# The division in the memory softmax of a two-layer decoder, moved from VectorE to ScalarE

## The reference

```python
def memory_branch(q_mem, mem, norm_mem, w_mem_kv):
    k_m, v_m = jnp.split(rmsnorm(mem, norm_mem) @ w_mem_kv, 2, axis=-1)
    q, k, v = _heads(q_mem, N_MEM_HEADS), _heads(k_m, N_MEM_HEADS), _heads(v_m, N_MEM_HEADS)
    sc = jnp.einsum('bqhd,bkhd->bhqk', q, k).astype(jnp.float32) * HEAD_DIM ** -0.5
    p = jax.nn.softmax(sc, axis=-1)
    o = jnp.einsum('bhqk,bkhd->bqhd', p.astype(v.dtype), v)
    return o.reshape(q_mem.shape)
```

## Time and profile before

| | |
|---|---|
| median of three runs | 1313.81 us (1313.54 to 1314.25) |
| profiled execution | 1317.49 us |
| its span, first to last instruction | 1315.7 us |
| TensorE busy | 1236.4 us, 94% |
| VectorE busy | 794.0 us, 60% |
| ScalarE busy | 555.4 us, 42% |
| GpSimd busy | 105.6 us, 8% |
| mean granted clock of TensorE | 0.976 |

### The profile page before, as it was taken

The page is one execution under the profiler, slowest core; times in us unless marked ns, Lnnn a source line. Parts: engine busy times, 40 slices in busy tenths (PEclk is TensorE's granted clock), DMA queues, the critical chain, the costliest instruction groups (busy, mean ns, idle before and its releaser), DMA issues.

```text
span 1315.7 us, 16934 instructions
## 1 busy us (share of the span) xinstructions
PE 1236.4 (94%) x5975; PEld 1014.6 (77%) x5975; DVE 794.0 (60%) x1235; ACT 555.4 (42%) x918; POOL 105.6 (8%) x133
## 2 busy tenths in 40 slices
PE   5889999989999999999999897777999999999998
PEld 4767888768788888878887676666878888887886
DVE  4866666654777777732267566554477777775225
ACT  5536656644444444421254442423344444442223
POOL 0201333332000000000020000000300000000000
PEclk9989999999999999999999897898999999999999
DMA  7412121113333333323321221111333333332642
GB/s 227 129 32 64 50 65 49 49 41 89 97 96 96 96 96 96 97 95 97 127 64 52 61 67 47 49 49 33 97 88 100 98 97 96 96 96 82 161 123 83
DMA packets 183893, 112.50 MB, mean 86 GB/s; under 512 B 20063, under 2 KB 176031, under 8 KB 183839
## 3 DMA queue, kind: packets, MB, share of 16 engines
q1 hardware_dynamic: 183838, 111.79, 28.9%
HBM read 107.58 MB, written 2.10 MB: 83 GB/s over the span
## 4 chain that ended last, share of the span: by engine, by line
PE 83%; DVE 11%; ACT 3%; issue 2%; DMA 1%; POOL 0%; SPq 0%; DVEq 0%; ACTq 0%; POOLq 0%
PE bank L1281 17%; PE bank L1283 17%; PE bank L1282 17%; PE bank L1569 7%; PE bank L1542 7%; PE bank L1433 2%; PE bank L1434 2%; PE bank L1435 2%; DVE w_lo L848 2%; PE bank L1555 2%; PE bank L1491 2%; PE bank L1582 1%; PE bank L1691 1%; PE bank L1469 1%; PE bank L1509 1%
## 5 line engine op out<-in xcount | busy, mean ns | idle before, releaser
L1281 PE MATMUL bank<-y_hi,w_hi 128*128 128x512 f32 x928 | 367.6, 396 | 2.8 <-DVE w_lo L848 2.5
L1282 PE MATMUL bank<-y_lo,w_hi 128*128 128x512 f32 x928 | 363.2, 391 | 0.0
L1283 PE MATMUL bank<-y_hi,w_lo 128*128 128x512 f32 x928 | 363.1, 391 | 0.0
L556 ACT ACTIVATE w_hi<-raw 128x1024 fp32r<-128x1024 f32 x186 | 196.5, 1056 | 355.5 <-PE bank L1283 180.1
L848 DVE TENSOR_TENSOR w_lo<-raw,w_hi 128x1024 fp32r<-128x1024 f32 x188 | 229.9, 1223 | 160.3 <-ACT w_hi L556 157.7
L1281 PEld LDWEIGHTS bank<-y_hi,w_hi 128*128 128x128 f32 x928 | 175.5, 189 | 41.8 <-issue 4.7
L1282 PEld LDWEIGHTS bank<-y_lo,w_hi 128*128 128x128 f32 x928 | 175.5, 189 | 37.0 <-issue 1.2
L1283 PEld LDWEIGHTS bank<-y_hi,w_lo 128*128 128x128 f32 x928 | 175.3, 189 | 36.9
L1542 PE MATMUL bank<-ar,w_hi 128*128 (+1 forms) x288 | 88.8, 389 | 0.8 <-DVE af L1066 0.8
L715 ACT ACTIVATE af<-af,conv 128x512 f32<-128x512 f32 x88 | 63.0, 716 | 36.0 <-DVE af L1066 36.0
L1569 PE MATMUL bank<-w_hi,ar 128*128 128x512 f32 x288 | 77.1, 390 | 0.8 <-DVE af L1066 0.8
(11 more groups left out here) (189 smaller groups left out, 1638.1 us busy)
## 6 DMA issues: line engine op xcount, KB each, us to landing
raw<-in_a_ffn_up SPq DMA_DIRECT2D x44, 512.0 KB, 3.8
raw<-in_b_ffn_up SPq DMA_DIRECT2D x44, 512.0 KB, 3.8
raw<-in_a_ffn_down SPq DMA_DIRECT2D x22, 512.0 KB, 3.3
raw<-in_b_ffn_down SPq DMA_DIRECT2D x22, 512.0 KB, 3.7
raw<-in_a_w_in SPq DMA_DIRECT2D x20, 512.0 KB, 3.8
raw<-in_w_kv_shared SPq DMA_DIRECT2D x12, 512.0 KB, 3.9
raw<-in_a_w_out SPq DMA_DIRECT2D x8, 512.0 KB, 3.8
raw<-in_b_w_in SPq DMA_DIRECT2D x8, 512.0 KB, 3.9
```

The costliest lines, as they stand in the source:

```text
L556: nc.scalar.activation(w_hi[:, m % SPLIT, :], raw[:, m % RAW, :], ACT.Copy).then_inc(hi_done, 1)
L1281: mm(bank, w[0], y[0][:, k, :], start=(k == 0), stop=False)
L1282: mm(bank, w[0], y[1][:, k, :], start=False, stop=False)
L1283: last = mm(bank, w[1], y[0][:, k, :], start=False, stop=(k == KT - 1))
```

## The change

The four multiplications leave VectorE. VectorE takes the reciprocals and signals them by a new semaphore `mrcp`; ScalarE waits for it directly behind its four exponentials, and then does four copies of 128 x 256 in place, with the reciprocal as scale. The last copy raises `mpn`. Before the reciprocals of a later head VectorE waits for the copies of the head before. The place in the program of everything else stays.

```diff
+        mrcp = sem("mrcp")
...
                     nc.scalar.activation(pm[:, M * qt:M * (qt + 1)], banks[2 + qt // 2][:, M * (qt % 2):M * (qt % 2) + M],
                                          ACT.Exp, bias=st[:, 8 + qt:9 + qt],
                                          accum_out=st[:, 12 + qt:13 + qt]).then_inc(mexp, 1)
+                act.wait_ge(mrcp, i + 1)
+                for qt in range(TT):
+                    ins = nc.scalar.activation(pm[:, M * qt:M * (qt + 1)], pm[:, M * qt:M * (qt + 1)], ACT.Copy,
+                                               scale=st[:, 16 + qt:17 + qt])
+                ins.then_inc(mpn, 1)
...
                     dve.wait_ge(mexp, 4 * (i + 1))
-                    link(nc.vector.reciprocal(st[:, 16:20], st[:, 12:16]))
-                    for qt in range(TT):
-                        ins = nc.vector.tensor_scalar(pm[:, M * qt:M * (qt + 1)], pm[:, M * qt:M * (qt + 1)],
-                                                      st[:, 16 + qt:17 + qt], None, ALU.mult)
-                    ins.then_inc(mpn, 1)
+                    if i:
+                        dve.wait_ge(mpn, i)
+                    nc.vector.reciprocal(st[:, 16:20], st[:, 12:16]).then_inc(mrcp, 1)
```

## The result

The changed kernel takes 1319.70 us (median, 1319.15 to 1320.30), the kernel before 1313.81 in the same comparison: ratio 1.0039, 95% interval 1.0026 to 1.0051, so 3.4 to 6.7 us slower (the two medians alone differ by 5.9 us, or 1.0045). Two later comparisons gave 1.0070 (1.0055 to 1.0085) and 1.0049 (1.0036 to 1.0063). The sign and the size of some 6 us hold in all three; the first two intervals don't overlap, and why is a part of what follows.

A forecast was written before the change was run, and what follows sets the result against it. The chain of waits, mostly on VectorE and ScalarE, was taken to bound the memory stretches, TensorE what follows. Layer B's 3.3 plus layer A's 2.5 gave 5.8 us, added to the median 1313.8: 1319.6 us; range 1316.0 to 1323.5.

The forecast's parts named there:

- layer A's term: Layer A's four slots: delays of 0.25, 0.91, 0.51 and 0.90 us, 2.5 us at the last head's values.
- The price of a copy: ScalarE's scaled 128 x 256 copies: 0.40 us from start to start, 0.50 for one; four have landed after 1.70.
- The slots with a tile: Where a filling tile ends, `w_lo` waits for ScalarE's delayed copy to `w_hi`: t + 2.90, some 0.90 to 1.03 us later.
- The slots without: Where no tile ends, TensorE's transposes wait for the probabilities: t + 1.92 instead of t + 1.41, 0.51 us later.
- Layer B: Layer B's four slots: delays of 0.90, 0.51, 0.90 and 1.03 us, together 3.3 us.
- rival 1: Longer pause before layer A's slot 3 transposes lowers TensorE's clock: 2 us more or somewhat over, 1321.5 to 1323; chance 0.18.
- The clock in layer B: Layer B's low-clock stretch may cover less of the work behind the pauses: up to 2 us back, 1317.6; chance 0.12.
- Half arrives: VectorE's gained time is used, or the stage behind a stretch returns part: about 2.5 us slower, 1316.3; chance 0.12.
- VectorE's lead: In each slot VectorE's step behind the removed multiplications can start about 1.07 us earlier; forecast as spent waiting.
- Engine time alone: Rule pricing only ScalarE's copies against VectorE's multiplications: 0.56 us in each of eight slots, 4.5 us slower.
- Faster: At `w_lo` in five slots with a tile, less VectorE work wins up to 4 us, 1309.8; chance 0.04.
- Dearer copies: ScalarE's scaled copies cost toward the upper end, 0.61 and 0.71 us: 1323 to 1326; chance 0.06.

The follow-up runs named there:

- the double copies: Changed kernel with each set of four scaled copies done twice, the second by a scale of 1.0 behind a wait; median 1335.54 us, ratio 1.0156.
- the pause filled: Changed kernel plus seven extra matmuls with unused results in TensorE's pause before the transposes of layer A's slot 3; median 1320.58 us, ratio 1.0045.
- layer B alone: Kernel before with the change made only in layer B, layer A still multiplying on VectorE; median 1317.26 us, ratio 1.0019.
- The split: Against the kernel before, VectorE multiplies three quarters and ScalarE copies one quarter with the scale; median 1314.38 us, ratio 0.9992.
- the two halves: Kernel before with the change in one layer only, two kernels: layer A 1317.63 us (1.0023), layer B 1317.26 us (1.0019).

## Why the prediction was right, and by how much that was luck

The mechanism was right: the copies delay ScalarE's queue and the probabilities by the forecast distances. That the total met the measurement to 0.1 us was luck: layer A's term was too small by some 1.9 us, and about as much was won outside the two stretches. 1319.6 was forecast and 1319.7 measured; the later comparisons, 9.1 and 6.6 us of difference, would have given 1322.9 and 1320.4 on the same base. All are in the range of 1316.0 to 1323.5. Point by point:

- **The price of a copy.** Forecast 0.40 from start to start, 1.70 for four; measured 1.70 or 1.71. The distance that was taken from the slope between 384 and 512 columns held to a hundredth. ScalarE is free 1.82 after the reciprocals, as forecast.
- **The slots with a tile.** `w_lo` 2.90 after the reciprocals was forecast; 2.89 to 2.91 in all five. VectorE's idle time before it, 1.77 to 2.13 us, stands where there had been none. Shown by the double copies as well (4.63).
- **The slots without.** Transposes at t + 1.92 forecast, 1.97 measured. The 0.05 that lay between the last multiplication and the transposes before (1.36 and 1.41) was left out of the forecast.
- **Layer B**: 3.3 forecast, 3.40 measured. From one reciprocal to the next the slots grew by 0.90, 0.57 and 0.89, and the last part, up to the values, by 1.04.
- **Layer A**: 2.5 forecast, 4.3 to 4.5 measured in three of the four profiles and 6.0 in the fourth. This term was mis-sized, because the clock was only a rival there. With the pause filled the stretch is 32.29, 2.49 over the mean of 29.80, so the queue's part has the size that was forecast. Within it slot 0 gave 0.10 over its mean instead of 0.25 and the end 0.91 instead of 0.76, which cancel: the transposes of slot 0 wait for TensorE's filling in the kernels without the change (1.68 to 2.22 after the reciprocals in four profiles), and the forecast read one of them. The rest of the surplus is the fall of the clock that rival 1 had described, with the mechanism and the place right (the pause before the transposes of slot 3, from 1.06 to 1.96 us) and a price of 1.8 to 2.0 us in three profiles and 3.5 in the fourth. It was given a chance of 0.18 and came in four profiles of four.
- **What paid for it.** In the first pair of profiles, after reached mark 1 by 1.45 us sooner, with less of a low stretch at 73 to 79 us, and was 1.7 faster between the marks. The second goes with the clock: of the fourteen profiles, the nine with 593.9 to 594.0 us there have a granted clock of 0.93 from 276 to 300 us, and the five with 592.2 to 592.4 have 1.00. Of each the row of one, before and then after:

```profile
284.00:288.00 4.00, 4.00 (x11) 3.13 (x12) 3.38 (x4) 1.88 (x3) 1.44 (x2) 0.57 0.46 134
```

```profile
284.00:288.00 4.00, 2.23 (x10) 1.50 (x9) 2.99 (x4) 3.14 (x4) 0.61 (x1) 1.00 0.00 0
```

  The changed kernel itself has both, 592.30 and 592.29 in two profiles and 593.88 in the third, so one execution can draw either; the rest differs by up to 3 us in the same way. Whether the change makes the shorter one likelier is open: the five profiles with all multiplications of layer A on VectorE have 593.9 to 594.0, and five of the other nine have 592.2 to 592.4. In the forecast these stood as nothing. The two stretches of after are 7.7 us longer than those without the change (66.88 against 29.80 + 29.35), the medians differ by 5.9, so 1.8 us were won outside them in the first comparison. The parts above are of that size, but no profile shows an execution of before near that comparison's median, so that they did it is argued and not shown.
- **Against the forecast's statement on the profile.** The two spans differ by 2.2 us, the medians by 5.9. To add the sum to the median and not to the one profiled execution was the step that kept the forecast right; the profiled execution of before was on the slow side of its own spread.
- **The rivals.** The clock in layer B, up to 2 us back (0.12): no; from the last values to the first filling behind them it is 5.02, 6.24 and 6.31 us in the three profiles of the changed kernel, 6.20 and 4.97 in the two of before. Half arrives (0.12): no, the distances show that VectorE's lead was not used, and layer B alone cost 2.8 us by the medians. Engine time alone, 0.56 for each head, would give 2.24 in layer B's stretch; 3.40 were measured. Faster (0.04): no; VectorE's lead of 1.07 us was spent waiting, as the bracket in the timeline shows. The split shows what a gain would need: a fourth of the copies on ScalarE, not all, and even that is seen in the stretches alone. Dearer copies (0.06): no.

What stays open: why the second comparison was 9.1 us, while the two halves beside it add up to 6.0. Its runs of the changed kernel go from 1321.1 at a mean clock of 0.976 to 1326.3 at 0.971, and the rest behind layer B was 2.8 us longer in its profile than in the first, with a lower granted clock there; that points to the clock, but the first profile of before has the same, so the change alone doesn't make it, and no experiment set the clock of that part. That the median of the kernel with seven matmuls fell by 0.55 and not by the 1.9 of its stretch is open for the same reason.

## What to carry to other kernels

Before moving work to an idler engine, read what stands behind it in that engine's queue and who waits for that: here ScalarE, busy for 42%, could not take 1.6 us in a slot without sending VectorE into a wait of 2.1 and TensorE's transposes 0.56 later. Share a step between two engines up to the point at which both hand over at the same time, rather than move it. And a chain of a few us across engines leaves pauses on TensorE; price the work behind them with the clock at both levels, and try to fill them.

## What the runs showed that was not expected

Matmuls whose results nobody reads make this kernel faster: 26 of them in three pauses are worth 3.2 us (0.9978, 0.9968 to 0.9987), and 25 with the split 6.2 us (0.9956, 0.9942 to 0.9970). The pauses were 1.6 to 3.1 us. And executions of one kernel on one chip differ by up to 6 us (1312.1 to 1318.5) where the first comparison showed a spread of 0.9, with the mean granted clock going the other way; a profile of one execution is a draw from that.
